# Mixture-of-experts decoder layer in fp32: the last two experts interleaved, their output taken by column halves and row tiles, and the two spare weight buffers loaded and used at other places

## What is computed

```python
t = rmsnorm(x, norm_moe)
logits = t @ w_router + b_router
combine = softmax weights of the top 4 of 32 experts, zero elsewhere
for w1, b1, w2, b2, ce in 32 experts:
    u = t @ w1 + b1
    g = minimum(u[:, :1024], 7); lin = clip(u[:, 1024:], -7, 7)
    a = g * sigmoid(1.702 * g) * (lin + 1)
    acc += ce[:, None] * (a @ w2 + b2)
out = rmsnorm(x + acc) * norm_final
```

## Time and profile before

| | us |
|---|---|
| median of three runs | 1325.38 (1324.53 to 1325.70) |
| the profiled execution's own time | 1324.43 |
| its span, first to last instruction | 1322.5 |
| TensorE busy | 1291.5 (98%) |
| VectorE, ScalarE busy | 411.8, 322.4 |
| HBM read | 473.42 MB, 359 GB/s over the span |

### The profile page before, as it was taken

One profiled execution on the slowest core, in us unless ns is written; L12 is line 12 of the kernel. 1 busy time (PEld: TensorE's weight loads), 2 busy tenths in 40 slices (PEclk: granted clock), 3 DMA queues, 4 the chain that ended last, 5 costly groups with the idle time before them and its releaser, 6 DMA issues.

```text
span 1322.5 us, 15133 instructions
## 1 busy us (share of the span) xinstructions
PE 1291.5 (98%) x6183; PEld 661.0 (50%) x6183; DVE 411.8 (31%) x736; ACT 322.4 (24%) x499; POOL 32.3 (2%) x42
## 2 busy tenths in 40 slices
PE   9999999999999999999999999999999999999997
PEld 9888888888886333333333333333333333333332
DVE  6765675545655121112111121111121111112112
ACT  5665455645443010101110010100011010001012
POOL 4000000000102000000000000000000000000000
PEclk9999999999999999999999999999999999999999
DMA  9554553636589999999999999999999999999996
GB/s 330 193 185 147 177 186 128 230 127 247 188 328 429 430 431 430 431 432 431 432 430 432 431 432 432 431 431 432 431 432 430 432 432 431 430 430 431 429 431 271
DMA packets 68031, 475.12 MB, mean 359 GB/s; under 512 B 7505, under 2 KB 9617, under 8 KB 43409
## 3 DMA queue, kind: packets, MB, share of 16 engines
q1 hardware_dynamic: 65840, 473.28, 86.2%
q10 hardware_dynamic: 2144, 1.21, 0.3%
HBM read 473.42 MB, written 1.05 MB: 359 GB/s over the span
## 4 chain that ended last, share of the span: by engine, by line
PE 79%; DMA 19%; DVE 0%; issue 0%; ACT 0%; SPq 0%; DVEq 0%; ACTq 0%
PE bank L1760 40%; DMA place<-in_w_exp_in 19%; PE bank L1569 18%; PE bank L1548 5%; PE bank L1878 4%; PE bank L1549 2%; PE bank L1556 1%; PE bank L1843 1%; PE bank L1773 1%; PE bank L1783 1%; PE bank L1761 1%; PE bank L1819 1%; PE bank L1692 1%; PE bank L1711 1%; PE bank L1520 0%; DMA ring<-in_w_in 0%
## 5 line engine op out<-in xcount | busy, mean ns | idle before, releaser
L1760 PE MATMUL bank<-place,fxqT 128*64 128x512 f32 x1520 | 677.3, 596 | 20.1 <-DMA place<-in_w_exp_in 19.1
L1761 PE MATMUL bank<-place,fxqT 128*64 128x512 f32 x1520 | 677.6, 596 | 0.0
L1760 PEld LDWEIGHTS bank<-place,fxqT 128*64 128x64 f32 x1520 | 198.4, 137 | 428.5 <-issue 389.0
L1761 PEld LDWEIGHTS bank<-place,fxqT 128*64 128x64 f32 x1520 | 198.4, 137 | 0.0
L1024 DVE TENSOR_TENSOR w_lo<-ring,w_hi 128x2048 fp32r<-128x2048 f32 x63 | 145.1, 2303 | 78.4 <-ACT w_hi L689 78.2
L689 ACT ACTIVATE w_hi<-ring 128x2048 fp32r<-128x2048 f32 x63 | 120.8, 1917 | 128.8 <-PE bank L1569 117.4
L1368 DVE TENSOR_SCALAR bank<-bank 128x512 f32<-128x512 f32 x32 | 22.4, 700 | 391.1 <-PE bank L1761 391.1
L1569 PE MATMUL bank<-w_hi,h_cat 128*128 128x512 f32 x448 | 141.1, 391 | 0.0
L933 ACT ACTIVATE fxqT<-bank 128x512 f32<-128x512 f32 x32 | 19.1, 597 | 413.6 <-DVE bank L1368 413.6
L1569 PEld LDWEIGHTS bank<-w_hi,h_cat 128*128 128x128 f32 x448 | 84.1, 188 | 17.4
L1359 DVE TENSOR_TENSOR fxqT<-bank,g_rows 128x256 f32<-128x256 f32 x64 | 24.2, 420 | 216.0 <-PE bank L1773 216.0
(11 more groups left out here) (291 smaller groups left out, 1071.0 us busy)
## 6 DMA issues: line engine op xcount, KB each, us to landing
place<-in_w_exp_in SPq DMA_DIRECT2D x125, 2048.0 KB, 36.7
place<-in_w_exp_out SPq DMA_DIRECT2D x63, 2048.0 KB, 37.4
ring<-in_w_in SPq DMA_DIRECT2D x19, 2048.0 KB, 7.6
ring<-in_w_branch SPq DMA_DIRECT2D x6, 2048.0 KB, 7.6
ring<-in_w_mem_kv SPq DMA_DIRECT2D x4, 2048.0 KB, 7.7
ring<-in_w_out SPq DMA_DIRECT2D x2, 2048.0 KB, 11.1
spare<-in_w_exp_in SPq DMA_DIRECT2D x2, 2048.0 KB, 12.1
ring<-in_w_in SPq DMA_DIRECT2D x2, 1024.0 KB, 7.6
```

The source lines that it names most:

```text
L1760: mm(o[0:CAP, :], lhsT, low, start=start, stop=stop)
L1761: return mm(o[CAP:P, :], lhsT, high, start=start, stop=stop)
```

## The change

1. **Spares.** `LOOPED` goes from 5 to 4: the loop runs four turns, twelve experts are written out instead of seven, and the spares hold pieces 120 and 121, the first two of expert 20. The load of `spare1` moves from the end of the mixing stage to just behind `load_ahead(3)` at unit 21, behind a wait for the last exponential of the forgetting attention. `spare0` stays. Two buffers of the mixing stage (`big_a`, `big_c`) swap their addresses to make that legal.
2. **Order of the last two experts.** The eight `w1` pieces of experts 30 and 31 are loaded and used first, then `w2` of 30, then `w2` of 31.
3. **Halves.** The `w2` of expert 31 is loaded in column halves: columns 0 to 511 of both pieces (1 MB each), then columns 512 to 1023 of the first (1 MB) and of the second in two parts of 512 KB. The matmuls have 256 output columns instead of 512. Each half is kept in a 128x512 tile with zeros in two blocks, and put with matmuls over all 128 rows (`put_late`).
4. **The end by halves and tiles.** The squares and the multiplication with `norm_final` of the first column half are made while the second is still multiplied. `norm_final` comes as one row of 4 KB and is spread over the partitions by a matmul with a row of ones in experts 22 and 23.

```diff
-LOOPED = NE // TURN - 1
+LOOPED = NE // TURN - 2
 SPARE_PIECE = LOOPED * TURN * PIECES
+LAST_TWO = (NE - 2) * PIECES
+LAST_ORDER = [(NE - 2 + n // W1, n % W1) for n in range(2 * W1)] + [(NE - 2 + n // W2, W1 + n % W2) for n in range(2 * W2)]
+GFIN_AT = (LOOPED * TURN + 2, LOOPED * TURN + 3)
+GFIN_BEHIND = GFIN_AT[0] * PIECES + RING_PLACES // 2
...
                     sp.wait_ge(proj_done, FIRST["caq"] + 3)
                     load_ahead(3)
+                    sp.wait_ge(exp_ready, 2 * FX_H)
+                    load_spare(1)
...
             sp.wait_ge(dve_drained, dve_drains(LAST_B2))
-            for b in range(SPARES):
-                load(SPARE_PIECE // PIECES, SPARE_PIECE % PIECES + b, RING_PLACES + b)
+            load_spare(0)
...
+                for j in range(W2):
+                    load_chunk(j, 0, slice(0, 4), place_in[late_turn(r, NE - 1, W1 + j)[0]])
+                load_chunk(0, 1, slice(0, 4), late_in[0])
+                for n in range(2):
+                    load_chunk(1, 1, slice(2 * n, 2 * n + 2), late_in[1 + n])
...
+            def last_two(r):
+                e = NE - 2
+                n = r * NE + e
+                layer_one(n, lambda j: late_turn(r, e, j))
+                pe.wait_ge(selWT_ready, n + 1)
+                gather(n * 2 + 4)
+                put(n)
+                turn_gathered(n + 2, RESULT)
+                pe.wait_ge(act_ready, n + 1)
+                turn_acts(acts, TURNS)
+                add_biases(r, n + 1)
+                pe.wait_ge(gotT_ready, (n + 2) * 2)
+                add_late_bias(r, n)
+                layer_one(n + 1, lambda j: late_turn(r, e + 1, j))
+                pe.wait_ge(aT_ready, n + 1)
+                layer_two(0, *late_turn(r, e, W1))
+                turn_weighted(r, n)
+                pe.wait_ge(act_ready, n + 2)
+                turn_acts(acts_late, GATE)
+                pe.wait_ge(pick_out_ready, n + 2)
+                add_half_bias(LINEAR, 0)
+                pe.wait_ge(selWT_ready, n + 2)
+                turn_weighted(r, n + 1)
+                pe.wait_ge(aT_ready, n + 2)
+                add_half_bias(GATE, 1)
+                layer_two(1, *late_turn(r, e, W1 + 1))
...
+                pe.wait_ge(place_in[b0], used0 * 16 + 16)
+                chunk(bank[LINEAR], b0, 0, range(4), 0, False)
+                put(n + 1)
+                pe.wait_ge(place_in[b1], used1 * 16 + 16)
+                chunk(bank[LINEAR], b1, 1, range(4), 0, True).then_inc(chunk_done, 1)
+                pe.wait_ge(late_in[0], r * 16 + 16)
+                chunk(bank[GATE], b0, 0, range(4), 1, False).then_inc(place_used[b0], 1)
+                put_late(r, 0)
+                for h in range(2):
+                    pe.wait_ge(late_in[1 + h], r * 16 + 16)
+                    ins = chunk(bank[GATE], b1, 1, range(2 * h, 2 * h + 2), 1, h == 1)
+                ins.then_inc(place_used[b1], 1)
+                put_late(r, 1)
...
+            def put_late(r, h):
+                pe.wait_ge(selWT_late_ready, r + 1)
+                pe.wait_ge(yS_late_ready, r * 6 + 2 * (h + 2))
+                for t in range(TT):
+                    ins = mm(sums[:, t, h, :], selWT_late[:, t, :], yS_late[h], start=False, stop=True)
...
+                    for t in range(TT):
+                        act.wait_ge(put_done, 4 * NE + 2 * (t + 1))
+                        act.activation(final_dump[:, t, :], sums[:, t, 1, :], ACT.Square,
+                                       accum_out=ss[:, t, 1:2]).then_inc(final_sq, 1)
+                        root(t)
...
+                    dve.wait_ge(early_kept, 2)
+                    for t in range(TT):
+                        reciprocal(t)
+                        if t == 0:
+                            scale_half(0, 0)
+                        dve.wait_ge(final_sq, t + 1)
+                        dve.scalar_tensor_tensor(out=results[:, t, UW:D], in0=sums[:, t, 1, :], scalar=rstd[:, t, 0:1],
+                                                 in1=gfin[:, UW:D], op0=ALU.mult, op1=ALU.mult).then_inc(final_ready, 1)
```

More of the change, by code:

```diff
@@ L242, in build @@
         gsig = big_a[:, 0:2 * D].rearrange("p (t d) -> p t d", t=TT)
+        big_c = part("big_c", [P, KT * (S + 3)])
+        pre = big_c[:, :].rearrange("p (c s) -> p c s", c=KT)
         clock = part("clock", [P, P])
@@ L408, in piece_turn, with late_turn, for_experts @@
             return b, r * place_uses(b) + used
-        def is_last(m, q):
-            return isinstance(m, int) and m * TURN + q == NE - 1
-        def for_experts(eng, r, expert):
+        def late_turn(r, e, j):
+            return piece_turn(r, LOOPED, LAST_TWO + LAST_ORDER.index((e, j)) - SPARE_PIECE)
+        def for_experts(eng, r, expert, last_two):
             with eng.Fori(0, LOOPED) as m:
@@ L418, in for_experts @@
                     expert(r, m, q)
-            for q in range(NE - LOOPED * TURN):
+            for q in range(NE - 2 - LOOPED * TURN):
                 expert(r, LOOPED + q // TURN, q % TURN)
+            last_two(r)
         def moe_turned(q, t):
@@ L464, in load, with load_spare @@
                 dst = place[b][:, :, :].rearrange("p k n -> p (k n)")
[L465 to L475, removed]
+                sp.dma_start(dst, src).then_inc(place_in[b], 16)
+            def load_spare(b):
+                load(SPARE_PIECE // PIECES, SPARE_PIECE % PIECES + b, RING_PLACES + b)
             def load_ahead(b):
@@ L1872, in put, with turn_acts, turn_weighted @@
-            def put(k, last=False):
+            def turn_acts(src, b):
+                for g in range(4):
+                    ins = pe.transpose(bank[b][:, P * g:P * (g + 1)], src[:, P * g:P * (g + 1)], ident[:, :])
+                ins.then_inc(act_turned, 1)
+            def turn_weighted(r, n):
+                pe.wait_ge(selW_ready, n * 2 + 2)
+                for t in range(TT):
+                    ins = pe.transpose(bank[TURNS][:, P * t:P * (t + 1)],
+                                       selW[:, t, :, :].rearrange("p o c -> p (o c)"), ident[:, :])
+                ins.then_inc(selT_done, 1)
@@ L1874, in put @@
+            def put(k):
                 pe.wait_ge(selWT_ready, k + 1)
@@ L1877, in put @@
                     t, half = q // 2, slice(CAP * (q % 2), CAP * (q % 2 + 1))
-                    mm(bank[SUMS + q][:, :], selWT[half, t, :], yS[half, :], start=False, stop=last).then_inc(put_done, 1)
+                    mm(bank[SUMS + q][:, :], selWT[half, t, :], yS[half, :], start=False, stop=False).then_inc(put_done, 1)
             def add_tokens():
@@ L1897, in experts @@
             def experts(r):
-                for_experts(pe, r, expert)
-                put((r + 1) * NE + r, last=True)
+                for_experts(pe, r, expert, last_two)
             for_rounds(pe, first_tokens, experts, read_late=True)
```

372 lines of the change are left out of this document (222 added, 150 removed).

## The result

The changed kernel takes **1327.95 us** (median of 13 runs, 1327.64 to 1328.86), the one before 1325.01 on the same chip (13 runs, 1324.43 to 1325.70). The ratio is 1.0023, with an interval of 1.0016 to 1.0030. It is 2.9 us slower. The forecast was 1325.3, no change, with a range up to 1327.2.

The account below looks back on a forecast made before the run. Bound by when the weight stream, transfer engines full, reaches its fourth piece from the end, and the work behind it. -0.55 + 2.45 - 2.0 = -0.1: 1324.3 on the profiled execution, 1325.3 as median; range 1323.4 to 1327.2 us.

Parts of the forecast that it names:

- Part 1a: Earlier spare1 load: a landing 1.6 us earlier and a 3 us idle stretch, 1.05 given back, net -0.55.
- The load of 413: Weight load issued at 413.10 when TensorE ends the projections: lands at 420.4 to 420.8 instead of 422.2.
- Part 1b: Spares at expert 20, five more experts written out: extra instruction packets cost 1.4 each or nothing; taken as nothing.
- rival B: Weight stream: later instruction packets hit a lagging engine once more, 1.4 us more, 1326.7, twice 1328.1; chance 0.22.
- Parts 2 and 3: Last two experts, from the fourth piece from the end to the last put's start: +2.45, ends +1.5 and +4.
- Rival D: Matmul steps of 256 columns cost more than half, weight loads not hidden: about 1329.5 us; chance 0.04.
- Part 4: Last put's start to span's end: 7.9 us instead of 9.94, with 3.0 to landing; gain 2.0, ends 1.5 and 2.3.

Follow-up runs that it names:

- spare1 early: Kernel before with only the load of spare1 moved to unit 21 and the two mixing buffers swapped: 1324.57 against 1324.91 us, ratio 1.0002.
- both parts: Kernel before with spare1 loaded early and four loop turns, the last experts as before: 1325.75 against 1325.06 us, ratio 1.0006.
- four turns alone: Kernel before with only LOOPED lowered to four turns, twelve experts written out, spares at expert 20: 1326.55 against 1324.91 us, ratio 1.0014.
- Six turns: Kernel before with the loop running six turns, two experts written out, spares at expert 30: 1333.39 against 1324.91 us, ratio 1.0066.
- the kernel with five turns: Changed kernel with LOOPED put back to five turns, spares at expert 25, norm_final in experts 27 and 28: 1329.27 against 1324.91 us, ratio 1.0035.

## Why the prediction was wrong

**Part 1a: the mechanism held, one size was off.** The load of 413 lands 7.2 after its issue (forecast 7.3 to 7.7), 1.6 earlier, and the rate has its hole. The first packet that catches the unbroken stream took 1.31, not 1.05. The 1.05 was read from the lift at 417.3, which belonged to a stream that had just begun to be full; most lifts of over 1 us in the full stream afterwards were between 1.3 and 1.5 (1.31, 1.29, 1.32 after; 1.51 and 1.35 with spare1 early; 1.33, 1.42, 1.42 with both parts). The term was -0.3 instead of -0.55.

**Part 1b is where the first step failed.** "By the above each costs 1.4 or nothing. I take nothing." It cost the 1.4: four turns alone are 1.6 slower, and in the changed kernel there is a third lift. This was rival B with one hit, at 0.18. The argument against it, that seven packets had cost one lift, already said that twelve or thirteen would cost about two; "nothing" was the weaker reading of that row. Six turns show the other side: without packets there is no lift. With part 1a beside it the loss is +0.7 by the medians, with an interval that reaches from no change to 2.0. The rule of the Trainium skill, "Runtime: NRT & Kernel Launch", section "Instruction fetch mechanics", that the fetching of blocks is mostly hidden was set against the two late landings. So far as TensorE goes the trace agrees: of its idle time from 420 us to its last matmul none is put down to "issue", before and after. It disagrees on the cost once the transfer engines are full: 1.3 to 1.5 us in a landing.

In the same part the prices of `norm_final` (0.9 + 0.7 each in experts 22 and 23) left out the clock, which fell to 0.50 behind each of the two matmuls. The lead hid that too, as no wait for a transfer stands between 957 and 1211 us, but the sign was wrong: waits vanished for over seven experts, not three or four. In the kernel with the old tail they return at 1124. The error had no part in the time.

**Parts 2 and 3 were right to 0.3.** +2.78 for +2.45. The bias and turns took what was said, and the first put took 1.91 for 1.9. What was missing are small things: the first matmul behind a put takes 0.36 and not 0.21 (1308.23, 1313.75), and the copy of half a tile took 0.44 for 0.38. TensorE waited 1.3 ahead of the first `w2` piece of expert 30 (forecast 1.6) and for no cut load. Rival D falls. A chunk of eight 256-column steps took 1.9 at most, the weight load of 0.14 hidden under 0.21. The Trainium skill, "TensorE: Matmul & The Clock Gate", section "Part 3: Packing small matmuls — row/col tiling", has loads overlap only where the row groups differ; the trace doesn't agree, at 256 columns as little as at 512.

**Part 4 is the second step that failed**, in "then 3.0 to landing". All the computing came as forecast: from the put's start to the last issue 4.6 (1316.25 to 1320.85) for 4.4. The transfer took 4.6 for 3.0. In both kernels a packet of 16 KB passes 5.3 us after the last put's start (1317.88 before, 1321.59 after, the latter for 1.7 us). Before, the last transfer was issued at 1319.04, 6.5 after the put's start, when it had passed nearly. The shorter chain issues it after 4.6, and the packet falls on it. So most of what part 4 saved in computing, the last transfer gave back. The gain of 2.0 shrank to 0.4. That the packets make the transfer 4.6 long is shown by the change without the code for further rounds (2.7 us, 2.0 faster), that crowding by tile 0 doesn't, by the run without it (4.5 us). But the 9.94 of before that the forecast started from held some 1.6 of the same kind (a last transfer of 3.0 for 2.0, and the stop of VectorE inside the last scaling). Without the code in either kernel part 4 gains 1.2. So the packets explain the miss of 1.6 against the forecast, but only some 0.5 of the 2.9 between the two kernels.

**The sum.** Forecast -0.55 + 0 + 2.45 - 2.0 = -0.1. Measured by the medians: parts 1a and 1b together +0.7, the tail +2.2. One reading beside the sum was off and had no part in it: by the earlier trace rows TensorE stands still 1.5 us an expert (5.2 of 100), not two.

**What stays open.** Which packet hits which transfer engine was not seen, since no row names the engine of a single packet. The runs show only that the lifts stand at the same places in two kernels with the same code ahead of the tail, each a few us behind a packet, and that there are none in the one kernel without packets. Why an undisturbed last transfer takes 2.7 in the change and 2.0 before was not followed up. No version beat the kernel before for the whole task: spare1 early alone is equal within its interval, and the one that is 1.5 faster by the medians lacks the code for more than 64 tokens. No run took the `norm_final` matmuls out of the change, so what their slow clock costs in the kernel with five turns is read from the trace alone.

## What to carry to other kernels

Once the transfer engines are full, code is no longer free: each instruction block that passes may hold back a landing by 1.3 us for good, so writing out five experts more has a price of its own (1.6 us here). A shortened tail must be looked at together with what passes when the engines leave their code; a final jump can put its packets right under the last output transfer. But the same effect must be priced in the kernel before as well, or it explains too much. A stall of TensorE costs more than the time it stands: in two kernels the steps behind a stall of 4.0 us took twice as long for over 5 us, and waits further on that would have covered the stall did not cover both. And buffers that run ahead are worth their lead only where enough of the stream follows: the same two spares at expert 30 made the kernel 8.5 us slower.

## What the runs showed of the hardware

- With instruction packets passing, a full stream of 431 GB/s lost 1.1 to 1.6 us in a single landing one to three times in 900 us, or in some kernels in several steps of 0.2 to 1.3. Without packets for 720 us there was no such loss.
- A taken branch ahead of the last experts stopped TensorE for 4.0 us, the same in two kernels. Behind it the granted clock was 0.50 (1.2 GHz) up to 5.3 and 5.7 us after work went on, and a 512-column step took 0.86 us for 0.43.
- The same level was granted behind the `norm_final` matmul over one row of the array and a wait of 0.8 us, twice in the change, and in its kernel with five turns behind one of the two.
- A 256 KB output transfer took 2.0 to 2.7 us in the kernels without the jump. As the last one it took 3.0 in the kernel before and 4.5 to 4.6 in the change with packets of 16 KB there, 3.5 with those of 8 KB alone.
- Weights of 64 columns loaded anew for every 256-column matmul left the pace at 0.21 us, half of 0.43. Only the first matmul behind a put took 0.15 more.
